# The recurrence of a hybrid encoder step: one copy of the front's rows for both halves, in three buffers

## The chip, the cores and the metric

The kernel is one launch on one core of a Trainium2 chip. The metric is the device time of the launch in microseconds (us); lower is better. PE is TensorE's matmul row and PEld its weight loads, DVE is VectorE, ACT is ScalarE, POOL is GpSimd. SP issues most DMAs.

## What is computed

A trunk of one layer runs over 2,048 tokens of a new stream and 16 tokens of each of eight running streams, all in float32. The input is normed and modulated, projected, mixed by two recurrences side by side, projected back, and sent through a mixture of experts. The change is in the recurrences:

```python
# HGRN2, 4 heads of 128 x 128:
#   S_t = diag(f_t) S_{t-1} + k_t v_t^T,   o_t = S_t^T q_t
# RWKV-7, 8 heads of 64 x 64:
def step(S, inp):
    r_t, lw_t, k_t, v_t, kk_t, a_t = inp
    sa = jnp.einsum('bhij,bhj->bhi', S, -kk_t)
    S = (S * jnp.exp(lw_t)[:, :, None, :]
         + sa[..., None] * (kk_t * a_t)[:, :, None, :]
         + v_t[..., None] * k_t[:, :, None, :])
    y = jnp.einsum('bhij,bhj->bhi', S, r_t)
    return S, y
```

Both outputs are normed by head, gated and laid side by side as `mix`, 1,024 wide.

## The kernel before

The program has four stages, one behind the other: `project`, `recur`, `merge` and `experts`. `project` leaves its results in HBM, with the channels on the rows: `rk`, for each group of 128 channels five kinds of rows (`RK_A0`, `RK_A1`, `RK_B0`, `RK_B1`, `RK_V`), `hk` with ten, and `tm`, by token. `recur` works through 17 tiles of 128 tokens, each made of two chunks of 64. Tiles 0 to 15 are the prompt; tile 16 (`TAIL`) holds the eight running streams.

A tile goes through two halves. The **front** of tile f needs no state: from `rkf` it turns V, B0 and B1 into token order (`turn`), multiplies B0 and B1 with A0 and A1 (`products`), and solves a triangular system by levels (`make_y`, `turn_x`, `make_x`), with the scores of the HGRN2 heads from `hkf` put between them (`score`). The **back** of tile b brings in the state: `from_state` multiplies A0 with the state, `solve` and `to_state` carry the state on, `y_from_state` multiplies A1 with it, and VectorE makes `mix`. The loop runs the front of tile i together with the back of tile i-1 in an order written out by hand, the same on each engine. I call one turn of this loop step i: it begins when the scores and the last transposes of the turn before are done.

The tiles of data have two buffers each, by the parity of the tile: `rkf` (all five kinds of rk, 10 KB in each partition), `hkf` (20 KB), and for the back `arb` (A0 and A1 once more, 4 KB), `qbb` and `tmb`. The front reads `rkf[f % 2]`. A whole step later the back reads A0 and A1 of the same tile, when `rkf[f % 2]` already belongs to another tile, so it has them loaded a second time into `arb`.

All of these loads are issued by SP, in the order of its program, and each waits at SP until its buffer is free:

```python
for i in range(TAIL + 1):
    if i + 2 <= TAIL:
        eng.wait_ge(ev("product_made"), 4 * i + 4)
        load_rk(i + 2)
        eng.wait_ge(ev("kd_made"), i + 1)
        load_hk(i + 2)
    b = i - 1
    if b >= 0:
        eng.wait_ge(ev("mixed"), b + 1)
        ...
```

`product_made` counts PE's products of the front, which come early in a step; `kd_made` is the last transposes of a front, and marks the end of a step; `mixed` is DVE's last operation on the mix of a tile, just behind it. By the clock a step thus begins with hk for the step after, the store of `mix`, the back's loads (`load_back`), and then rk for two steps ahead.

Of the tail, `ard`, `qbd`, `vd`, `hd` and `SAd` are masked copies that lie in buffers no longer needed (`hkf[1]` and `rkf[1]`). ScalarE writes the squares of o to `osq` and of y to `ysq`, and DVE sums them.

Of the kernel before, what the change touches and what calls it, by code (L numbers as in the profile page):

```python
# [21 lines left out]
PT = SEQ // 128  # L22
# [864 lines left out]
def recur(nc, t, bonus, ends):  # L887

    names = []
    with ExitStack() as ctx:  # L890
# [10 lines left out]

        const = sb("const", [128, N_CONST, 128])
# [4 lines left out]
        rkf = [sb(f"rkf{p}", [128, 4, N_RK, 128]) for p in range(2)]  # L907
        hkf = [sb(f"hkf{p}", [128, 4, N_HK, 128]) for p in range(2)]
        arb = [sb(f"arb{p}", [128, 4, 2, 128]) for p in range(2)]
# [17 lines left out]
        osq = sb("osq", [128, 512])  # L927
# [3 lines left out]
        ysq = sb("ysq", [128, 512])  # L931
# [12 lines left out]
        hd = [rkf[1][:, n, 0:4, :].rearrange("p a b -> p (a b)") for n in range(2)]  # L944
        SAd = [rkf[1][:, 2 + n, 0:4, :].rearrange("p a b -> p (a b)") for n in range(2)]
# [9 lines left out]

        TAIL = PT
# [8 lines left out]
        def chunk(c):  # L965
            return slice(CH * c, CH * c + CH)
# [43 lines left out]
        def _(eng):  # L1010
            eng.dma_start(ident, t["const"][:, 128 * C_ID:128 * C_ID + 128]).then_inc(ev("ident_in"), 16)

            def load_rk(f):

                k, p = 128 * f, f % 2
                for c in range(4):
                    eng.dma_start(rkf[p][:, c, :, :], rk3[:, c, :, k:k + 128]).then_inc(ev(f"rk_in{p}"), 16)
# [11 lines left out]
            def load_back(f):  # L1029

                k, p = 128 * f, f % 2
                for c in range(4):
                    eng.dma_start(arb[p][:, c, :, :], rk3[:, c, RK_A0:RK_A1 + 1, k:k + 128]).then_inc(ev(f"back_in{p}"), 16)
                eng.dma_start(qbb[p][:, :, :], hk3[:, :, HK_B, k:k + 128]).then_inc(ev(f"back_in{p}"), 16)
                eng.dma_start(tmb[p][:, :, :].rearrange("p a b -> p (a b)"), t["tm"][k:k + 128, :]).then_inc(ev(f"back_in{p}"), 16)
# [7 lines left out]
            load_back(1)  # L1043
            eng.dma_start(even[:, :, :].rearrange("p a b -> p (a b)"), t["even"]).then_inc(ev("state_in"), 16)
# [5 lines left out]
            for i in range(TAIL + 1):  # L1050
                if i + 2 <= TAIL:
                    eng.wait_ge(ev("product_made"), 4 * i + 4)
                    load_rk(i + 2)
                    eng.wait_ge(ev("kd_made"), i + 1)
                    load_hk(i + 2)
                b = i - 1
                if b >= 0:
                    eng.wait_ge(ev("mixed"), b + 1)
                    eng.dma_start(t["mix"][128 * b:128 * b + 128, :], mix[b % 2][:, :]).then_inc(ev(f"mix_out{b % 2}"), 16)
                    if b + 2 <= TAIL:  # L1060
                        load_back(b + 2)
# [17 lines left out]
        def _(eng):  # L1079
# [3 lines left out]
            def h_update(b):  # L1083

                p = b % 2
                eng.wait_ge(ev(f"back_in{p}"), 96 * (b // 2 + 1))
# [95 lines left out]
            def turn(f, kind, bank):  # L1182

                p = f % 2
                for c in range(4):
                    ins = eng.transpose(bank[:, 128 * c:128 * c + 128], rkf[p][:, c, kind, :], ident)
                ins.then_inc(ev("tok_made"), 1)

            def product(f, kind, banks, h, c):

                p, o = f % 2, 128 * (h // 2)
                return eng.matmul(banks[h % 2][chunk(c), o:o + 128].rearrange("p (a b) -> p a b", a=2), rkf[p][half(h), h // 2, kind, chunk(c)],
                                  rkf[p][half(h), h // 2, RK_A0:RK_A1 + 1, chunk(c)], start=(h < 2), stop=(h >= 6), skip_group_check=True)
# [129 lines left out]
            for i in range(TAIL + 1):  # L1323
# [8 lines left out]
                eng.wait_ge(ev(f"rk_in{p}"), 64 * (f // 2 + 1))  # L1332
# [137 lines left out]
        def _(eng):  # L1470
# [46 lines left out]
            for i in range(TAIL + 1):  # L1517
# [9 lines left out]
                if back:  # L1527
                    eng.wait_ge(ev("o_made"), b + 1)
                    eng.activation(osq[:, :], P_O[:, :], ACT.Square).then_inc(ev("o_squared"), 1)
# [11 lines left out]
                for lv in range(2, levels(f)):  # L1541
                    if back and lv == 5:
                        y_root(b)
                    keep_xt(f, lv - 1)
                    if back and lv == min(4, levels(f) - 1):
                        eng.wait_ge(ev("y_centred"), b + 1)
                        eng.activation(ysq[:, :], yc[:, :], ACT.Square).then_inc(ev("y_squared"), 1)
                    if lv < levels(f) - 1:
                        keep_x(f, lv)
# [11 lines left out]
            eng.activation(osq[:, :], P_O[:, :], ACT.Square).then_inc(ev("o_squared"), 1)  # L1561
# [13 lines left out]
            eng.activation(ysq[:, :], yc[:, :], ACT.Square).then_inc(ev("y_squared"), 1)  # L1575
# [9 lines left out]
        def _(eng):  # L1585
# [89 lines left out]
            def o_variance(b):  # L1675

                eng.wait_ge(ev("o_squared"), b + 1)
                step(eng.tensor_reduce(hst[:, 0, :], heads(osq[:, :], 4), AX.X, ALU.add))
                settle()
                eng.tensor_scalar(hst[:, 1, :], hst[:, 0, :], 1.0 / 128, NORM_EPS, ALU.mult, ALU.add).then_inc(ev("o_var"), 1)  # L1680
# [26 lines left out]
            def y_variance(b):  # L1707

                eng.wait_ge(ev("y_squared"), b + 1)
                step(eng.tensor_reduce(rst[:, 1, :], heads(ysq[:, :], 8), AX.X, ALU.add))  # L1710
# [67 lines left out]
            eng.wait_ge(ev(f"back_in{p}"), 96 * (TAIL // 2 + 1))  # L1778
# [841 lines left out]
```

## Time and profile before

| | |
|---|---|
| median of 3 runs | 3234.86 us (3229.3 to 3235.49) |
| the profiled execution | 3231.98 us |
| its span | 3230.2 us |
| PE busy | 2943.0 us, 91% |
| PEld busy | 1735.1 us, 54% |
| DVE, ACT, POOL busy | 44%, 30%, 5% |
| bytes moved by DMA | 575.75 MB, mean 178 GB/s |
| mean granted clock of TensorE | 0.956 |
| stage `recur` | about 1107 to 1800 us |

The span is the time from the first to the last instruction that the profile holds; the execution's own time is 1.8 us longer. "Busy" adds up the instructions of an engine; the weight loads run beside the matmuls. A wait is given with its releaser, the engine and line that ended it; "issue" stands where the profile shows nothing that was waited for.

### The profile page before, as it was taken

Reading aid. Unit: us, or ns where it says so; the run is one execution under the profiler, and the core shown is the slowest. Engines: PE = TensorE matmul, PEld = TensorE weight load, DVE = VectorE, ACT = ScalarE, POOL = GpSimd, SP = SyncE. Lnnn points to the kernel's source line nnn. Section 1 sums busy time; section 2 is a strip of 40 time slices with the busy share of each in tenths; the row PEclk is TensorE's granted clock in tenths of the full one; section 3 lists DMA queues with packets and bytes.
Section 4 is the critical chain, followed back from the end, with each engine's and each line's share of the span. In section 5 each row is a group of like instructions: output and inputs, shape, how many; then the busy total and the mean of one; then the engine's idle time right before and its main releaser. Section 6 shows DMA issues by size and latency. Waiting matters only on the chain. (4 is left out here: it accounts for less than half of the span.)

```text
span 3230.2 us, 68743 instructions
## 1 busy us (share of the span) xinstructions
PE 2943.0 (91%) x28939; PEld 1735.1 (54%) x28940; DVE 1410.5 (44%) x3438; ACT 974.7 (30%) x1872; POOL 162.0 (5%) x248
## 2 busy tenths in 40 slices
PE   6998999999999488888898599949999999999988
PEld 2432455454555378778787355535555555555543
DVE  2245466665655545666666144451221122212217
ACT  2456334343334223333332122102222212222215
POOL 0000000000000000000000000001011001111104
PEclk8999999999999789999999699979999999999998
DMA  7531123242332586555661643465786478767758
GB/s 270 209 130 56 50 93 116 92 138 85 109 132 86 163 220 181 155 153 156 173 181 37 213 162 115 152 170 205 286 323 255 152 262 308 254 230 276 253 196 332
DMA packets 373371, 575.75 MB, mean 178 GB/s; under 512 B 31246, under 2 KB 231110, under 8 KB 370088
## 3 DMA queue, kind: packets, MB, share of 16 engines
q1 hardware_dynamic: 335112, 470.72, 43.2%
q0 software_dynamic: 18080, 72.10, 6.4%
q10 hardware_dynamic: 19968, 29.83, 3.2%
q8 instruction: 168, 2.75, 0.4%
q14 instruction: 43, 0.35, 0.0%
HBM read 427.04 MB, written 145.54 MB: 177 GB/s over the span
## 5 line engine op out<-in xcount | busy, mean ns | idle before, releaser
L451 PE MATMUL pj_P<-pj_hT,pj_wc 128*128 128x448 f32 (+2 forms) x1600 | 592.0, 517 | 0.9 <-ACT pj_stage L579 0.9
L2493 PE MATMUL moe_PG<-wgu,moe_xT 128*64 128x256 f32 x5248 | 582.1, 380 | 0.7 <-ACT moe_xT L2391 0.7
L2493 PEld LDWEIGHTS moe_PG<-wgu,moe_xT 128*64 128x64 f32 x5248 | 377.5, 137 | 226.0 <-issue 47.2
L451 PEld LDWEIGHTS pj_P<-pj_hT,pj_wc 128*128 128x128 f32 x1600 | 294.8, 189 | 257.5 <-issue 241.2
L2500 PE MATMUL moe_PTY<-wd,moe_hT 128*64 128x512 f32 x1312 | 317.7, 603 | 0.0
L2394 ACT ACT_TABLE_LOAD x82 | 105.2, 1283 | 483.1 <-issue 483.0
L1978 PE MATMUL merge_PO<-merge_w,merge_mT 128*128 128x512 f32 x544 | 240.9, 601 | 1.6 <-DMA merge_w<-in_w_out 1.6
L1978 PEld LDWEIGHTS merge_PO<-merge_w,merge_mT 128*128 128x128 f32 x544 | 103.3, 192 | 126.6 <-issue 123.9
L2357 DVE COPY moe_hT<-moe_PH 128x128 f32<-128x128 f32 x164 | 47.8, 292 | 281.0 <-PE moe_PH L2485 281.0
L2353 DVE TENSOR_TENSOR moe_sg<-moe_sg,moe_PG 128x128 f32<-128x128 f32 x164 | 46.4, 283 | 282.7 <-ACT moe_sg L2394 282.7
L2360 DVE COPY moe_y<-moe_PTY 128x512 f32<-128x512 f32 x82 | 56.7, 692 | 208.3 <-PE moe_PTY L2500 208.3
L2500 PEld LDWEIGHTS moe_PTY<-wd,moe_hT 128*64 128x64 f32 x1312 | 81.9, 136 | 120.2 <-issue 86.8
L372 PE MATMUL pj_P<-pj_wt,pj_hT 128*128 128x512 f32 x272 | 122.9, 606 | 0.0
L482 PE MATMUL pj_P<-pj_wt,pj_hT 128*128 128x512 f32 x272 | 121.3, 599 | 0.0
L1300 PE MATMUL re_P<-re_hkf 128*64 128x64 f32 x1872 | 87.6, 237 | 10.7 <-issue 9.6
L600 ACT ACTIVATE pj_rk<-pj_P,pj_keep_mu 128x448 f32<-128x448 f32 (+1 forms) x60 | 35.9, 602 | 196.8 <-DVEq L866 91.6
L2396 ACT ACTIVATE moe_sg<-moe_PG 128x128 f32<-128x128 f32 x82 | 22.8, 278 | 234.3 <-PE moe_PG L2493 234.3
L1655 DVE COPY_PREDICATED re_Y<-re_const,re_P 128x256 f32<-128x256 uint32 x166 | 64.5, 442 | 54.9 <-PE re_P L1251 28.4
L1508 ACT COPY re_XT<-re_P 128x256 f32<-128x256 f32 x132 | 42.7, 375 | 148.2 <-PE re_P L1260 148.2
L482 PEld LDWEIGHTS pj_P<-pj_wt,pj_hT 128*128 128x128 f32 x272 | 50.3, 190 | 67.7 <-issue 67.7
L2441 POOL DMA_INDIRECT moe_xg<-scratch_h,moe_row x83 | 80.6, 971 | 67.1 <-POOL moe_row L2438 67.1
L372 PEld LDWEIGHTS pj_P<-pj_wt,pj_hT 128*128 128x128 f32 x272 | 51.8, 196 | 59.8 <-issue 59.8
(385 smaller groups left out, 4140.2 us busy)
## 6 DMA issues: line engine op xcount, KB each, us to landing
wgu<-in_w_gate SPq DMA_DIRECT2D x32, 2048.0 KB, 9.4
wgu<-in_w_up SPq DMA_DIRECT2D x32, 2048.0 KB, 15.0
wd<-in_w_down SPq DMA_DIRECT2D x32, 2048.0 KB, 16.6
re_hkf<-scratch_hk SPq DMA_DIRECT2D x60, 640.0 KB, 8.0
re_rkf<-scratch_rk SPq DMA_DIRECT2D x68, 320.0 KB, 6.6
scratch_hk<-pj_hk SPq DMA_DIRECT2D x16, 1344.0 KB, 5.8
scratch_y_rows<-moe_y ACTq DMA_DIRECT2D x164, 128.0 KB, 5.2
scratch_rk<-pj_rk SPq DMA_DIRECT2D x16, 1120.0 KB, 4.4
```

Source lines behind the costliest of these rows:

```text
L372: ins = eng.matmul(P[2 + m % 2][:, :], hT_cols(m)[:, k, :], wt[:, k, :], start=(k == 0), stop=(k == KD - 1))
L451: ins = eng.matmul(bank[:, 0:wp], wc[:, j, k, :], hT[:, k, k0:k0 + wp], start=(k == 0), stop=(k == KD - 1), skip_group_check=True)
L482: ins = eng.matmul(PQ[:, :], rows[:, k, :], wt[:, k, :], start=(k == 0), stop=(k == KD - 1))
L1300: ins = eng.matmul(P_ST[chunk(c), 256 + 64 * h:320 + 64 * h], hkf[p][:, h, a, chunk(c)], hkf[p][:, h, b, chunk(c)], start=(h == 0), stop=( ...
L1655: eng.copy_predicated(Y[lv - 1][:, 4 * g:4 * g + 4, :], level_mask(C_LEVEL_T, lv).bitcast(U32).unsqueeze(1).to_broadcast([128, 4, CH]), he ...
L1978: ins = eng.matmul(PO[:, half, :], mT[:, n % 2, k, :], w[:, k, 512 * half:512 * half + 512], start=(k == 0), stop=(k == KD - 1))
L2357: eng.tensor_copy(hT[:, j, :], PH[:, j, 0:128]).then_inc(ev("hT_kept"), 1)
L2360: eng.tensor_copy(y[:, :], PY[:, :]).then_inc(ev("y_kept"), 1)
L2394: eng.activation(sg[:, 0, :], PG[:, 0, 0:128], ACT.Sigmoid).then_inc(ev("sigmoid_made"), 1)
L2441: eng.indirect_dma_start(xg[:, :], None, t["h2"].rearrange("t (h c) -> (t h) c", h=2), bass.IndirectOffsetOnAxis(ap=row[:, 0:1], axis=0)). ...
L2493: ins = eng.matmul(PG[64 * c:64 * c + 64, j, 0:256].rearrange("p (a b) -> p a b", a=2), x_rows, wgu[p][:, :, k, o:o + 128], start=(k == 0) ...
L2500: ins = eng.matmul(PY[64 * n:64 * n + 64, :], hT[:, j, 64 * c:64 * c + 64], wd[p][:, 2 * c + j, 512 * n:512 * n + 512], start=(j == 0 and ...
```

## The change

- `rkf` has three buffers, chosen by `f % 3`, with a semaphore for each; `arb` is gone. `from_state` and `y_from_state` of the back read `RK_A0` and `RK_A1` in `rkf[b % 3]`, and so does the masked copy `ard` of the tail.
- `load_back` loads `qbb` and `tmb` only, so `back_in` counts 32 a tile, not 96.
- `load_rk(2)` is issued at the start, ahead of the running streams' states. In the loop `load_rk(i + 2)`, behind the fourth product, becomes `load_rk(b + 3)`, the same tile, behind the store of `mix` of tile b = i - 1 and ahead of `load_back`.
- `osq` and `ysq` are one buffer, `sq`. `hd` and `SAd` lie in `rkf[(TAIL + 1) % 3]`.

The SBUF space: a third `rkf` takes 10 KB a partition, `arb` gave back 8 KB and the squares 2 KB.

```diff
+        TAIL = PT
...
-        rkf = [sb(f"rkf{p}", [128, 4, N_RK, 128]) for p in range(2)]
+        rkf = [sb(f"rkf{p}", [128, 4, N_RK, 128]) for p in range(3)]
         hkf = [sb(f"hkf{p}", [128, 4, N_HK, 128]) for p in range(2)]
-        arb = [sb(f"arb{p}", [128, 4, 2, 128]) for p in range(2)]
...
-        osq = sb("osq", [128, 512])
+        sq = sb("sq", [128, 512])
...
-        ysq = sb("ysq", [128, 512])
...
-        hd = [rkf[1][:, n, 0:4, :].rearrange("p a b -> p (a b)") for n in range(2)]
-        SAd = [rkf[1][:, 2 + n, 0:4, :].rearrange("p a b -> p (a b)") for n in range(2)]
+        hd = [rkf[(TAIL + 1) % 3][:, n, 0:4, :].rearrange("p a b -> p (a b)") for n in range(2)]
+        SAd = [rkf[(TAIL + 1) % 3][:, 2 + n, 0:4, :].rearrange("p a b -> p (a b)") for n in range(2)]
...
-                    eng.dma_start(rkf[p][:, c, :, :], rk3[:, c, :, k:k + 128]).then_inc(ev(f"rk_in{p}"), 16)
+                    eng.dma_start(rkf[f % 3][:, c, :, :], rk3[:, c, :, k:k + 128]).then_inc(ev(f"rk_in{f % 3}"), 16)
...
-                for c in range(4):
-                    eng.dma_start(arb[p][:, c, :, :], rk3[:, c, RK_A0:RK_A1 + 1, k:k + 128]).then_inc(ev(f"back_in{p}"), 16)
                 eng.dma_start(qbb[p][:, :, :], hk3[:, :, HK_B, k:k + 128]).then_inc(ev(f"back_in{p}"), 16)
...
             load_back(1)
+            load_rk(2)
             eng.dma_start(even[:, :, :].rearrange("p a b -> p (a b)"), t["even"]).then_inc(ev("state_in"), 16)
...
             for i in range(TAIL + 1):
                 if i + 2 <= TAIL:
-                    eng.wait_ge(ev("product_made"), 4 * i + 4)
-                    load_rk(i + 2)
                     eng.wait_ge(ev("kd_made"), i + 1)
                     load_hk(i + 2)
                 b = i - 1
                 if b >= 0:
                     eng.wait_ge(ev("mixed"), b + 1)
                     eng.dma_start(t["mix"][128 * b:128 * b + 128, :], mix[b % 2][:, :]).then_inc(ev(f"mix_out{b % 2}"), 16)
+                    if b + 3 <= TAIL:
+                        load_rk(b + 3)
                     if b + 2 <= TAIL:
                         load_back(b + 2)
...
-                    ins = eng.matmul(out_g(chunk(c), h), arb[p][half(h), h // 2, 0, chunk(c)], ST[half(h), h // 2, :],
+                    ins = eng.matmul(out_g(chunk(c), h), rkf[b % 3][half(h), h // 2, RK_A0, chunk(c)], ST[half(h), h // 2, :],
...
-                    ins = eng.matmul(out_y(chunk(c), h), arb[p][half(h), h // 2, 1, chunk(c)], ST[half(h), h // 2, :],
+                    ins = eng.matmul(out_y(chunk(c), h), rkf[b % 3][half(h), h // 2, RK_A1, chunk(c)], ST[half(h), h // 2, :],
...
-                eng.wait_ge(ev(f"rk_in{p}"), 64 * (f // 2 + 1))
+                eng.wait_ge(ev(f"rk_in{f % 3}"), 64 * (f // 3 + 1))
...
-                step(eng.tensor_tensor(ard[n][:, :, :, :].rearrange("p m a c -> p (m a) c"), arb[p][:, :, :, :].rearrange("p m a c -> p (m a) c"),
-                                       cols.unsqueeze(1).to_broadcast([128, 8, 128]), ALU.mult))
+                step(eng.tensor_tensor(ard[n][:, :, :, :], rkf[TAIL % 3][:, :, RK_A0:RK_A1 + 1, :],
+                                       cols.unsqueeze(1).unsqueeze(1).to_broadcast([128, 4, 2, 128]), ALU.mult))
```

What moves is on SP alone; PE, DVE, ACT and POOL have the same instructions in the same order. First SP's start, from the back's loads of the second tile to the first store of `mix` (`even`, `even_row`, `Sd` and `srow` are the masks and the states of the running streams). Before:

```order
L1033 DMA re_arb1<-scratch_rk 128x2x128 x4
L1034 DMA re_qbb1<-scratch_hk 128x4x128
L1035 DMA re_tmb1<-scratch_tm 128x1536
L1044 DMA re_even<-in_even 128x256
L1045 DMA re_even_row<-in_even_row 128x2
L1046 DMA re_Sd<-in_state_hgrn 128x32x128
L1049 DMA re_srow<-in_state_rwkv 64x8x64 x8
L1017 DMA re_rkf0<-scratch_rk 128x5x128 x4
L1024 DMA re_hkf0<-scratch_hk 128x10x128 x4
L1017 DMA re_rkf1<-scratch_rk 128x5x128 x4
L1024 DMA re_hkf1<-scratch_hk 128x10x128 x4
L1059 DMA scratch_mix<-re_mix0 128x1024
```

After the change:

```order
L1031 DMA re_qbb1<-scratch_hk 128x4x128
L1032 DMA re_tmb1<-scratch_tm 128x1536
L1016 DMA re_rkf2<-scratch_rk 128x5x128 x4
L1042 DMA re_even<-in_even 128x256
L1043 DMA re_even_row<-in_even_row 128x2
L1044 DMA re_Sd<-in_state_hgrn 128x32x128
L1047 DMA re_srow<-in_state_rwkv 64x8x64 x8
L1023 DMA re_hkf0<-scratch_hk 128x10x128 x4
L1023 DMA re_hkf1<-scratch_hk 128x10x128 x4
L1055 DMA scratch_mix<-re_mix0 128x1024
```

rk of tile 2 (`rkf2`) now stands ahead of the states, and the two rk loads that stood around the first `hkf0` of the loop are gone from there. The other place is one step in the middle of the loop. Before:

```order
L1024 DMA re_hkf0<-scratch_hk 128x10x128 x4
L1059 DMA scratch_mix<-re_mix1 128x1024
L1033 DMA re_arb1<-scratch_rk 128x2x128 x4
L1034 DMA re_qbb1<-scratch_hk 128x4x128
L1035 DMA re_tmb1<-scratch_tm 128x1536
L1017 DMA re_rkf1<-scratch_rk 128x5x128 x4
L1024 DMA re_hkf1<-scratch_hk 128x10x128 x4
```

After the change:

```order
L1023 DMA re_hkf0<-scratch_hk 128x10x128 x4
L1055 DMA scratch_mix<-re_mix1 128x1024
L1016 DMA re_rkf1<-scratch_rk 128x5x128 x4
L1031 DMA re_qbb1<-scratch_hk 128x4x128
L1032 DMA re_tmb1<-scratch_tm 128x1536
L1023 DMA re_hkf1<-scratch_hk 128x10x128 x4
```

The four `arb` loads are gone, and the four rk loads that came last in the step stand between the store of `mix` and the loads of `qbb` and `tmb`.

## Rows read from the trace of the kernel before

**Rows 1.** The page: busy time of each engine, and the instruction queue (packets, MB, share).
```profile
PE 2943.0 (91%) x28939; PEld 1735.1 (54%) x28940; DVE 1410.5 (44%) x3438; ACT 974.7 (30%) x1872; POOL 162.0 (5%) x248
...
q8 instruction: 168, 2.75, 0.4%
```

**Rows 2.** Windows: us, busy (count) of PE, PEld, DVE, ACT, POOL; PEclk, DMA share, GB/s.
```profile
1107.00:1161.00 54.00, 29.26 (x720) 25.91 (x722) 14.10 (x35) 9.39 (x22) 0.00 (x0) 0.69 1.09 284
1161.00:1681.00 520.00, 461.59 (x13654) 417.31 (x13650) 317.49 (x724) 168.31 (x433) 0.00 (x0) 0.97 0.60 165
1681.00:1715.00 34.00, 32.17 (x980) 28.97 (x980) 23.13 (x54) 12.08 (x31) 0.00 (x0) 1.00 0.42 127
```

**Rows 3.** Waits of PE in steps 1 to 14: total us, times, longest us.
```profile
PE re_P L1251 <- issue: 10.2, 5, 2.8
PE re_P L1300 <- issue: 9.6, 9, 3.2
...
PE re_P L1240 <- issue: 0.2, 1, 0.2
```

**Rows 4.** Windows from one resumption of PE to the next, behind a burst.
```profile
1405.69:1409.71 4.02, 3.36 (x128) 3.02 (x128) 1.23 (x3) 1.29 (x4) 0.00 (x0) 1.00 0.02 5
1409.71:1413.83 4.12, 3.23 (x128) 2.75 (x127) 2.90 (x7) 1.80 (x5) 0.00 (x0) 1.00 0.02 4
```

**Rows 5.** Timeline of SP, one step: start us, us, issue.
```profile
1420.41 5.44 SPq L1024 DMA_DIRECT2D re_hkf<-scratch_hk  x4
1425.90 2.98 SPq L1059 DMA_DIRECT2D scratch_mix<-re_mix  x1
1428.92 3.04 SPq L1033 DMA_DIRECT2D re_arb<-scratch_rk  x4
1432.00 0.47 SPq L1034 DMA_DIRECT2D re_qbb<-scratch_hk  x1
1432.51 1.09 SPq L1035 DMA_DIRECT2D re_tmb<-scratch_tm  x1
1433.65 4.73 SPq L1017 DMA_DIRECT2D re_rkf<-scratch_rk  x4
```

**Rows 6.** Timeline of PE at the end of the gap: start us, us, work, idle before.
```profile
1441.59 0.58 PE L1251 MATMUL re_P<-re_X,re_LB 64*64 64x64 f32 x10 [2.84 <-issue]
```

**Rows 7.** DMA view of the burst, 1420.4 to 1442.4 us.
```profile
DMA packets 9709, 6.08 MB, mean 276 GB/s; under 512 B 239, under 2 KB 9450, under 8 KB 9706
q1 hardware_dynamic: 9706, 6.03, 99.5%
```

**Rows 8.** DMA view, 1434.5 to 1438.5, then 1438.5 to 1439.0 us.
```profile
DMA packets 1077, 1.25 MB, mean 313 GB/s; under 512 B 41, under 2 KB 949, under 8 KB 1077
q1 hardware_dynamic: 1077, 1.25, 99.6%
...
q8 instruction: 1, 0.02, 14.7%
```

**Rows 9.** Windows behind the gap of rows 6.
```profile
1442.00:1445.00 3.00, 3.00 (x87) 2.77 (x81) 1.54 (x4) 0.65 (x2) 0.00 (x0) 0.50 0.05 14
1445.00:1450.00 5.00, 4.75 (x188) 4.20 (x180) 3.62 (x9) 1.94 (x6) 0.00 (x0) 1.00 0.02 3
```

**Rows 10.** The tile rkf: what PE waited for (us, times), and its loads' time to land.
```profile
  DMA re_rkf<-scratch_rk: 26.4, 1
DMA to landing us min/median/max: 4.5/6.6/12.4
```

**Rows 11.** Step 1: SP's two rk loads, and PE's two gaps.
```profile
1161.29 3.46 SPq L1017 DMA_DIRECT2D re_rkf<-scratch_rk  x4
1172.92 6.52 SPq L1017 DMA_DIRECT2D re_rkf<-scratch_rk  x4
...
1179.32 0.27 PE L1135 MATMUL re_PEO<-re_ST,re_arb 64*64 64x64 f32 x2 [1.54 <-issue]
1184.27 0.91 PE L1177 MATMUL re_PEO<-re_SA,re_LB 64*64 64x64 f32 x24 [1.89 <-issue]
```

More of the change, by code:

```diff
@@ L943, in recur @@
         vd = [hkf[1][:, 2 + n, 4:8, :].rearrange("p a b -> p (a b)") for n in range(2)]
-        hd = [rkf[1][:, n, 0:4, :].rearrange("p a b -> p (a b)") for n in range(2)]
-        SAd = [rkf[1][:, 2 + n, 0:4, :].rearrange("p a b -> p (a b)") for n in range(2)]
+        hd = [rkf[(TAIL + 1) % 3][:, n, 0:4, :].rearrange("p a b -> p (a b)") for n in range(2)]
+        SAd = [rkf[(TAIL + 1) % 3][:, 2 + n, 0:4, :].rearrange("p a b -> p (a b)") for n in range(2)]
         P_A, P_B, P_C, P_D, P_ST, P_O = [ctx.enter_context(nc.psum_tensor(f"re_P{b}", [128, 512], F32)) for b in range(6)]
         P_EO = ctx.enter_context(nc.psum_tensor("re_PEO", [128, 2, 512], F32))
-        TAIL = PT
         AHEAD = {2: (), 3: (1,), 4: (3,), 5: (5,)}
@@ L1085, in h_update @@
                 p = b % 2
-                eng.wait_ge(ev(f"back_in{p}"), 96 * (b // 2 + 1))
+                eng.wait_ge(ev(f"back_in{p}"), 32 * (b // 2 + 1))
                 eng.wait_ge(ev("kdT_kept"), b + 1)
@@ L1185, in turn @@
                 for c in range(4):
-                    ins = eng.transpose(bank[:, 128 * c:128 * c + 128], rkf[p][:, c, kind, :], ident)
+                    ins = eng.transpose(bank[:, 128 * c:128 * c + 128], rkf[f % 3][:, c, kind, :], ident)
                 ins.then_inc(ev("tok_made"), 1)
@@ L1191, in product @@
                 p, o = f % 2, 128 * (h // 2)
-                return eng.matmul(banks[h % 2][chunk(c), o:o + 128].rearrange("p (a b) -> p a b", a=2), rkf[p][half(h), h // 2, kind, chunk(c)],
-                                  rkf[p][half(h), h // 2, RK_A0:RK_A1 + 1, chunk(c)], start=(h < 2), stop=(h >= 6), skip_group_check=True)
+                return eng.matmul(banks[h % 2][chunk(c), o:o + 128].rearrange("p (a b) -> p a b", a=2), rkf[f % 3][half(h), h // 2, kind, chunk(c)],
+                                  rkf[f % 3][half(h), h // 2, RK_A0:RK_A1 + 1, chunk(c)], start=(h < 2), stop=(h >= 6), skip_group_check=True)
             def products(f, kind, banks):
@@ L1528, in _ @@
                     eng.wait_ge(ev("o_made"), b + 1)
-                    eng.activation(osq[:, :], P_O[:, :], ACT.Square).then_inc(ev("o_squared"), 1)
+                    eng.activation(sq[:, :], P_O[:, :], ACT.Square).then_inc(ev("o_squared"), 1)
                 eng.wait_ge(ev("x0_made"), f + 1)
@@ L1546, in _ @@
                         eng.wait_ge(ev("y_centred"), b + 1)
-                        eng.activation(ysq[:, :], yc[:, :], ACT.Square).then_inc(ev("y_squared"), 1)
+                        eng.activation(sq[:, :], yc[:, :], ACT.Square).then_inc(ev("y_squared"), 1)
                     if lv < levels(f) - 1:
@@ L1560, in _ @@
             eng.wait_ge(ev("o_made"), TAIL + 1)
-            eng.activation(osq[:, :], P_O[:, :], ACT.Square).then_inc(ev("o_squared"), 1)
+            eng.activation(sq[:, :], P_O[:, :], ACT.Square).then_inc(ev("o_squared"), 1)
             eng.wait_ge(ev("as_made"), 2 * TAIL + 1)
@@ L1574, in _ @@
             eng.wait_ge(ev("y_centred"), TAIL + 1)
-            eng.activation(ysq[:, :], yc[:, :], ACT.Square).then_inc(ev("y_squared"), 1)
+            eng.activation(sq[:, :], yc[:, :], ACT.Square).then_inc(ev("y_squared"), 1)
             eng.wait_ge(ev("y_var"), TAIL + 1)
@@ L1677, in o_variance @@
                 eng.wait_ge(ev("o_squared"), b + 1)
-                step(eng.tensor_reduce(hst[:, 0, :], heads(osq[:, :], 4), AX.X, ALU.add))
+                step(eng.tensor_reduce(hst[:, 0, :], heads(sq[:, :], 4), AX.X, ALU.add))
                 settle()
@@ L1709, in y_variance @@
                 eng.wait_ge(ev("y_squared"), b + 1)
-                step(eng.tensor_reduce(rst[:, 1, :], heads(ysq[:, :], 8), AX.X, ALU.add))
+                step(eng.tensor_reduce(rst[:, 1, :], heads(sq[:, :], 8), AX.X, ALU.add))
                 settle()
@@ L1777, in _ @@
             p = TAIL % 2
-            eng.wait_ge(ev(f"back_in{p}"), 96 * (TAIL // 2 + 1))
+            eng.wait_ge(ev(f"back_in{p}"), 32 * (TAIL // 2 + 1))
             eng.wait_ge(ev("state_in"), 16 * (3 + NSEQ))
```

## The prediction

> **What bounds the kernel now.** I read the page first. TensorE is busy 91% of the span [rows 1]; the change touches one of four stages, the recurrence, so I cut that stage by its own clock. The table of windows [rows 2] gives its step 0 (1107 to 1161 us), steps 1 to 14 (1161 to 1681) and step 15 (1681 to 1715). In the 520 us of steps 1 to 14 the matmul row is busy 461.59 us, so TensorE paces the loop, and 58.4 us are idle: 37.1 us a step.
>
> The table of waits says what that idle time is. Almost none of it waits for another engine: the largest entries carry the releaser "issue", that is, for nothing that the profile shows [rows 3]; all thirteen such entries come to 48.9 us, 3.5 us a step. What they are is read from where they fall. Two resumptions after such a gap are 1405.70 and 1409.71, the next is 1413.84, and each interval holds 128 matmuls and as many weight loads, one short in one record [rows 4]. So TensorE stops after equal amounts of program, not at a given tensor. The queue called instruction moved 168 packets, 2.75 MB, 16 KB each [rows 1], and one packet goes for each such piece. These gaps are TensorE waiting for its own program. Between 1405.69 and 1413.83 data traffic is nil (share 0.02) and a piece still takes 4.0 to 4.1 us: the floor of that supply.
>
> Next the traffic. SP issues a step's loads in one go, from 1420.41 to 1438.4 [rows 5] (phase, below, is the time since the first of them), and the 22 us from there move 9,706 packets and 6.03 MB at 99.5% of the 16 engines [rows 7]. The rest of the step is empty (share 0.60 over the whole, [rows 2]). The large gap comes inside that burst: 2.84 us, ending at 1441.59 [rows 6]. From 1434.5 to 1438.5 all 1,077 packets are the data queue's, among them the 128 long rows of tmb (1,077 less the 949 under 2 KB); the packet that ends the wait went between 1438.5 and 1439.0 [rows 8]. So **the data burst delays the program, and TensorE pays**. After the gap the granted clock is 0.50 for 3 us (1.2 GHz of 2.4), 87 matmuls against 188 in the next 5 us [rows 9]: 29 per us for 37.6, some 0.7 us lost on top. The mean clock of 0.97 over 520 us [rows 2] makes 31 us at the lower level, ten such spells in fourteen steps.
>
> The proof by absence is step 15, which asks for no rk rows: share 0.42 of 34 us, 14.3 us busy instead of 22.3, and it lasts 33.9 us, 3.2 less than the mean step [rows 2].
>
> **The change part by part.**
> *The second read of A0 and A1 goes.* Four loads of 128 KB a step, 1,024 packets of 512 B, of 6.03 MB and 9,706 packets [rows 7]. By bytes at the 276 GB/s of that row 0.524 MB is 1.9 us, by packets 22 x 0.995 x 1,024 / 9,706 = 2.3 us. I take 2.0 us off each burst. What a shorter burst is worth has two bounds. Step 15 gives the lower: 8 us less burst gave 3.2 us, 0.4 per us, so 0.8 us a step. The upper is one for one, 2.0 us, since the gap ends about where the burst ends (21.2 us after the first issue, of a burst of some 22). I take **1.1 us** a step: 0.8 plus 0.3 for the clock (ten spells of 0.7 us are 0.5 a step; of these something over half should go with smaller gaps). It is nearer the lower bound, since step 15 is the nearest row, and since the packet that ends the gap goes some 3 us before the burst's end, where a burst cut by 2 us hardly reaches it.
>
> *The front's rk rows move.* Today they are the last loads of a step, for two steps ahead; now they come between the store of mix and the rows of qbb and tmb, for one step ahead. On SP four issues for four: rk (4.73 us) comes in, arb (3.04 us) goes out ahead of qbb and tmb [rows 5]. These two land some 2 to 4 us later, by about phase 20, and are wanted by the next step's first matmuls, at phase 37: covered by 17 us. rk is issued from phase 8.5 (5.44 + 2.98) and lands within 12.4 us at worst [rows 10], by 21 to 26, and the transposes of the next step want it: covered by over 10 us. Today TensorE waits for rk exactly once, at the very start, 26.4 us [rows 10], where its four loads stand first on SP before and after: nothing. If that cover were gone every step would wait; it would take a burst twice as long. SP's wait for the fourth product goes; behind it only rk stood. The wait on mixed has hk ahead of it and rk, qbb and tmb behind, and mixed is done by 1425.9, while hk is still being issued, so nobody waits for it longer than now.
>
> *Step 1 is relieved.* There two rk loads are issued today, at 1161.29 and 1172.92, and TensorE stops for 1.54 and 1.89 us at 1179.32 and 1184.27 [rows 11]. Now rk for step 2 goes ahead of the states during step 0 and rk for step 3 to step 2: **-3.0 us** of the 3.4. Step 0 trades two arb loads (-1.05 MB) for one of rk (+1.31 MB) in 54 us that are saturated anyway (284 GB/s, [rows 2]): 0, give or take 2.
>
> *Step 15 is loaded.* It now asks for the rows of step 16: +4.5 us of rk for -2 us of arb, at 0.4 to 1 per us +1 to +2.5; I take **+1.5 us**.
>
> *Squares, hd, SAd, the masked A rows.* One buffer for both squares: ScalarE writes the second only after y is centred, three levels after the first was summed, and both engines keep that order. The two masks read the same elements with another stride, and hd and SAd move to the buffer that is free. PE, DVE and ACT have the same rows in the same order, so the pieces of program break at the same matmuls. All 0, hidden or unchanged.
>
> Sum: -3.0 - 13 x 1.1 + 1.5 = **-15.8 us** on the profiled execution's 3231.98, so 3216; that execution stands 2.9 us under the median of 3234.86. Against the median: 3219; between the two I say **3218 us**. A measurement here tells some 0.2%, 6.5 us, from no change.
>
> The Trainium skill speaks against this ("Runtime: NRT & Kernel Launch", "Instruction fetch mechanics"): fetching is streamed ahead and hidden behind the issue of instructions. By that rule the gaps would be something else and the sum nothing. The trace disagrees: [rows 4] and [rows 8].
>
> **The rivals.**
> *The burst's end is what ends the gap.* For it: the end of the gap lies at 21.2 us in the step shown, and of a burst's length only the last part touches a gap. Then each step gains 2.0 us and the clock: -3 - 13 x 2.2 + 2.5 = -29, **3206 us**. Against it: step 15's 0.4 per us.
>
> *The loads are hidden; nothing moves.* The gap is set by which piece of program meets a full queue, and a step with 20 us of burst has as many pieces in it as one with 22. Then -3 + 1.5: **3233 us**. For it: gaps of 0.7 us also come with no traffic at all, at 1409.71 [rows 4], and a piece cannot come faster than 4.0 us; what is won in the burst can be lost behind it.
>
> *Slower: the long rows now stand last.* tmb's packets (6 KB) pass between phase 14 and 18 now, and no instruction packet passes beside them [rows 8]. After the change hk, mix, rk are issued with no lighter load between them and tmb closes the burst, just where the step's third piece is wanted. If a piece that asks at phase 16 must sit out rk's rest and tmb, its gap grows by about the length of tmb, 0.79 MB at 276 GB/s = 2.8 us, in the one step of three where the pieces fall so, less what the shorter burst saves (0.8): +2.0 x 13/3 = +9, and step 15 +2.5, step 1 -3: +8.2, **3243 us**. It decides from the point where the main gap's mean passes today's 3.5 us a step. The Trainium skill ("DMA: Bandwidth & Descriptors", "Queues, rings and completion order") lets an engine switch between queues only after a whole packet of several descriptors, which is this mechanism; by the trace such waits exist [rows 8].
>
> **How the numbers follow.** Forecast 0.52, one for one 0.14, hidden 0.21, slower 0.13. The forecast's own range, with 0.8 to 1.7 us a step, is 3208 to 3225. The range to hold 8 in 10 reaches into both neighbours: **3203 to 3237**. Faster by over 0.2% takes the forecast and the first rival, 0.66; within 0.2% the hidden one and the edges, 0.22; slower 0.12.
>
> **What would show it.** Right: no arb loads, 5.5 MB and some 20 us busy in a step's burst; "issue" gaps in steps 2 to 14 down from 3.5 to about 2.4 us a step; step 1 near 34 us, step 15 near 35.5; still one wait of TensorE for rk. Wrong: a second such wait; gaps as long as before at the burst's new end; or gaps that merely move behind tmb.

## The result, and the profile after

| | before | changed |
|---|---|---|
| median | 3235.49 us (5 runs, 3229.3 to 3245.67) | 3217.3 us (5 runs, 3215.24 to 3221.84) |
| ratio | | 0.9938, 95% interval 0.9920 to 0.9957 |
| profiled execution | 3231.98 us | 3221.84 us |
| its span | 3230.2 us | 3220.0 us |

The change makes the kernel faster by 18 us, 0.6%. The forecast was 3218 us. The total came out as forecast; the largest part, steps 2 to 14, was given its gain for the wrong reason, as the experiments show.

The profiled execution of the changed kernel is the slowest of its five. Behind the recurrence, from the first matmul of `merge` on, it takes 2.9 us longer than that of before, in code that is the same (before, then changed):

```profile
1809.95:3230.18 1420.23, 1332.86 (x8696) 706.16 (x8696) 418.39 (x1136) 309.62 (x568) 130.20 (x201) 0.97 0.65 232
```
```profile
1796.83:3220.00 1423.17, 1332.25 (x8696) 705.54 (x8696) 418.47 (x1136) 309.59 (x568) 129.88 (x201) 0.97 0.65 231
```

So the stage is read by itself. A step is cut at the first matmul that brings the values of HGRN2 into the state (`h_update`); columns as in [rows 2]. Step 1, steps 2 to 14 and step 15 before:

```profile
1161.90:1199.10 37.20, 32.91 (x980) 30.00 (x976) 20.85 (x50) 12.08 (x31) 0.00 (x0) 0.95 0.59 150
1199.10:1682.10 483.00, 428.88 (x12692) 387.48 (x12688) 297.70 (x677) 156.82 (x403) 0.00 (x0) 0.97 0.60 166
1682.10:1716.00 33.90, 32.07 (x980) 28.89 (x977) 23.03 (x53) 12.08 (x31) 0.00 (x0) 1.00 0.43 128
```

and in the changed kernel:

```profile
1163.10:1196.20 33.10, 31.39 (x980) 28.69 (x976) 20.99 (x50) 12.07 (x31) 0.00 (x0) 1.00 0.35 91
1196.20:1665.20 469.00, 423.87 (x12692) 381.06 (x12688) 297.99 (x677) 156.73 (x403) 0.00 (x0) 0.99 0.57 156
1665.30:1701.60 36.30, 32.38 (x978) 29.13 (x976) 23.07 (x53) 12.07 (x31) 0.00 (x0) 1.00 0.50 141
```

Steps 2 to 14 go from 483.0 to 469.0 us with the same 12,692 matmuls, step 1 from 37.2 to 33.1, step 15 from 33.9 to 36.3. Of the 14.0 us, 9.0 are idle time (54.1 us against 45.1 beside the matmul row) and 5.0 are busy time. I put that to the clock: the work is the same, and the mean granted clock rises from 0.97 to 0.99.

The waits of TensorE in the same 520 us as [rows 3] (total us, times, longest us):

```profile
PE re_P L1258 <- issue: 7.2, 10, 1.7
PE re_P L1298 <- issue: 6.7, 13, 0.9
PE re_P L1249 <- issue: 4.7, 8, 0.9
```

The entries "issue" come to 38.3 us where there were 48.9, and these 520 us now hold part of step 15 as well. In steps 2 to 14 alone they fall from 45.3 to 36.1 us, 3.5 to 2.8 a step, and to 32.5 us (2.5 a step) in the second profile of the change, `change_again` below. L1298 and L1249 are the L1300 and L1251 of before; their longest wait was 3.2 and 2.8 us and is 0.9 in this profile. Long gaps are not gone: one of 2.6 us is left, and the second profile has one of 2.9. SP's step, which answers to [rows 5]:

```profile
1409.60 5.44 SPq L1023 DMA_DIRECT2D re_hkf<-scratch_hk  x4
1415.08 3.63 SPq L1055 DMA_DIRECT2D scratch_mix<-re_mix  x1
1418.76 3.88 SPq L1016 DMA_DIRECT2D re_rkf<-scratch_rk  x4
1422.68 1.67 SPq L1031 DMA_DIRECT2D re_qbb<-scratch_hk  x1
1424.39 0.83 SPq L1032 DMA_DIRECT2D re_tmb<-scratch_tm  x1
```

The burst, to compare with [rows 7], in the 22 us from the first issue:

```profile
DMA packets 8628, 5.57 MB, mean 253 GB/s; under 512 B 176, under 2 KB 8368, under 8 KB 8624
q1 hardware_dynamic: 8624, 5.51, 91.5%
```

0.52 MB and 1,082 packets fewer, and 91.5% of the window in place of 99.5%, 20.1 us. And the tile `rkf`, to compare with [rows 10]:

```profile
  DMA re_rkf<-scratch_rk: 26.8, 1
DMA to landing us min/median/max: 4.7/5.9/14.1
```

One wait for rk, at the start, as before: the cover held.

### The profile page after: what moved, and what is told of

It is laid out like the page before. It is cut to its first block and busy times, and to the rows that moved or that the text cites. A ratio compares the mean times of both kernels' runs of the same rounds, so it can differ in the third digit from the quotient of the medians.

```text
span 3220.0 us, 68675 instructions
## 1 busy us (share of the span) xinstructions
PE 2938.7 (91%) x28939; PEld 1728.7 (54%) x28940; DVE 1411.6 (44%) x3438; ACT 974.2 (30%) x1872; POOL 161.3 (5%) x248
## 5 line engine op out<-in xcount | busy, mean ns | idle before, releaser
L2392 ACT ACT_TABLE_LOAD x82 | 105.2, 1283 | 483.0 <-issue 482.9
L600 ACT ACTIVATE pj_rk<-pj_P,pj_keep_mu 128x448 f32<-128x448 f32 (+1 forms) x60 | 35.9, 602 | 196.8 <-DVEq L866 91.7
L1298 PE MATMUL re_P<-re_hkf 128*64 128x64 f32 x1872 | 86.6, 234 | 7.8 <-issue 6.7
```

The costliest lines, as they stand in the source:

```text
L1298: ins = eng.matmul(P_ST[chunk(c), 256 + 64 * h:320 + 64 * h], hkf[p][:, h, a, chunk(c)], hkf[p][:, h, b, chunk(c)], start=(h == 0), stop=( ...
L2392: eng.activation(sg[:, 0, :], PG[:, 0, 0:128], ACT.Sigmoid).then_inc(ev("sigmoid_made"), 1)
```

## The experiments

Single profiled executions of one kernel differ by 5 to 10 us, so totals are compared by ratios, each with the kernel before on the same chip, and stages by several profiles. A second quantity is worked out from the trace. [rows 4] showed that TensorE's program comes in pieces of 256 instructions, one packet of the instruction queue for each. **The delay** below is the time from TensorE's first instruction of a piece to the start of the next packet of that queue, averaged over the pieces that begin in a given part of steps 2 to 14. With no data in flight it is 1.0 to 1.4 us.

The delay decides a gap. In the eight profiles of the kernel before, the change, `rk_last`, `arb_kept` and `rk_last_short` (the last three are explained below) TensorE has 244 gaps of over 0.3 us at the end of a piece in these steps. It resumes 2.5 us (median; all lie between 2.2 and 3.0) after the start of the packet, in each profile alike. So a piece takes its delay plus 2.5 us, or TensorE's own work on it where that is longer, and a gap is what the delay has over.

### Amount or place: two kernels that each do half of the change

The texts recorded ahead of the runs name the theories by letter: A, only the amount of traffic counts; B, only the place of the loads in the step; C, both; D, the long rows of tmb are what holds up the program.

`rk_last` keeps the three buffers and the lost arb loads, and puts rk back at the end of the step:

```diff
-                    if b + 3 <= TAIL:
-                        load_rk(b + 3)
                     if b + 2 <= TAIL:
                         load_back(b + 2)
+                    if b + 3 <= TAIL:
+                        load_rk(b + 3)
```

> The changed kernel with one thing put back: in the loop the rk loads stand last again, behind qbb and tmb; arb stays gone. Before, a step of steps 2 to 14 lasted 37.15 us, with the change 36.08. Theory A (only the amount of traffic counts): steps of 36.1 us, total as the changed kernel, about 3217 to 3219 us. Theory B (only the place of the long tmb rows counts, the lost arb traffic is worth nothing): steps of 37.1 us, total about 3231. Theory C (both count, as in the forecast: what delays the program is what stands in the DMA queues when TensorE asks for the next piece): between them, 36.4 to 36.8 us a step, total 3222 to 3227. Main gap of the step behind phase 14 back to 2 us or more under B, about 1 us under A.

`arb_kept` is the kernel before, with two buffers and arb, and rk ahead of the back's loads:

```diff
+                if i == 0:
+                    eng.wait_ge(ev("product_made"), 4)
+                    load_rk(2)
                 if i + 2 <= TAIL:
-                    eng.wait_ge(ev("product_made"), 4 * i + 4)
-                    load_rk(i + 2)
                     eng.wait_ge(ev("kd_made"), i + 1)
...
+                    if b + 3 <= TAIL:
+                        load_rk(b + 3)
                     if b + 2 <= TAIL:
                         load_back(b + 2)
```

> The kernel before with one thing changed: rk is issued between the store of mix and the back's loads, two buffers, arb still loaded (rk of tile 2 still in step 0 to 1, rk of tile 3 a step later). Theory A (amount only): steps 2 to 14 stay at 37.15 us, step 1 gains about 2 to 3 us and step 15 loses 2, total about 3234. Theory B (order only): steps of 36.1 us, total about 3220. Theory C (both): 36.5 to 36.9 us, total 3226 to 3231. If arb_kept and rk_last together give more or less than the change's 1.07 us a step, the two effects do not add.

The first time `rk_last` came to 0.9966 (0.9954 to 0.9978), 3229.33 against 3237.89 us, and `arb_kept` to 0.9930 (0.9908 to 0.9951), 3218.19 us from four runs. Both were run again beside the changed kernel, on one chip.

> The changed kernel once more, beside the next three on one chip, since single profiled executions of one kernel differ by some 5 to 10 us: 0.9938 again, some 20 us under the kernel before.

> rk last in the step, arb gone (traffic alone). First time 0.9966. If the place of the loads counts for about half, it lies 9 us over the changed kernel again, ratio 0.996 to 0.9975; if the first result was chance and only the amount counts, it meets the changed kernel at 0.994.

> rk ahead of the back's loads, arb kept (place alone). First time 0.9930 from 4 runs, as good as the whole change. Theory B (place alone is the change): 0.993 to 0.995 again, and the lost 8.9 MB of arb are worth under 4 us. Theory C (both): 0.996.

| one chip, before 3233.6 us | median us | ratio (95%) | steps 2 to 14 in its profile |
|---|---|---|---|
| the change (no arb, rk ahead) | 3211.78 | 0.9936 (0.9913 to 0.9959) | 465.3 us |
| rk_last (no arb, rk last) | 3228.47 | 0.9984 (0.9971 to 0.9997) | 477.8 us |
| arb_kept (arb, rk ahead) | 3222.54 | 0.9958 (0.9940 to 0.9976) | 477.7 us |

The lost traffic alone is worth 5 us by the medians (9 the first time), the new place alone 11 us (20 the first time), the two together 22 us. The changed kernel and `rk_last` differ in nothing but the order of six loads in a step, their intervals do not meet, and the medians lie 17 us apart. So theory A falls. By the medians place counts for most of it, but theory B does not hold in full: with arb kept the second time some 11 us are missing, though the intervals of these two overlap, and the two halves together (16 us) give less than the whole (22). How the sum divides is known no better than to these intervals. The single profiles divide it otherwise: in the table the two halves gain alike, and the first profiles had 485.2 us for `rk_last` and 475.4 for `arb_kept`. Two profiles of one kernel thus lie up to 7.4 us apart in these 13 steps. In profiles, `change_again`, `rk_last_again` and `arb_kept_again`:

```profile
1192.70:1658.00 465.30, 423.22 (x12692) 380.71 (x12688) 298.15 (x677) 156.66 (x403) 0.00 (x0) 0.99 0.57 158
```
```profile
1198.30:1676.10 477.80, 429.48 (x12692) 388.01 (x12688) 297.46 (x677) 156.75 (x403) 0.00 (x0) 0.97 0.56 153
```
```profile
1195.10:1672.80 477.70, 428.44 (x12691) 385.55 (x12689) 297.51 (x677) 156.81 (x403) 0.00 (x0) 0.98 0.61 168
```

### Why the place counts: the long rows of tmb

A step's piece that begins at phase 12 to 15 (phase: us from about the step's first hk issue) had to wait 3.2 us for the next packet in the kernel before (2.8 to 3.5 by where the edges of the bin are put), 3.6 and 3.7 in the two profiles of `rk_last`, but 2.1 and 2.0 in the two of the change and 2.1 in both of `arb_kept`, eight to ten pieces each. What passes then is tmb, with rows of 6 KB, in the slow ones, and rk, with rows of 512 B, in the others.

The long rows are not gone from the other kernels, they pass later. By their packets they go at phase 14 to 18 before, 12 to 16 in `rk_last`, 17 to 20 in the change, and 19 to 22 in `arb_kept`, where arb stands ahead of them. There the twelve pieces of the two profiles that begin at phase 18 to 19 wait 3.1 us, and the eleven of the change 1.3. So arb costs something by pushing tmb into that part of the step, and amount and place are not two separate terms.

`rk_last_short` takes `rk_last` and cuts tmb's rows:

```diff
-                eng.dma_start(tmb[p][:, :, :].rearrange("p a b -> p (a b)"), t["tm"][k:k + 128, :]).then_inc(ev(f"back_in{p}"), 16)
+                for j in range(6):
+                    eng.dma_start(tmb[p][:, :, :].rearrange("p a b -> p (a b)")[:, 256 * j:256 * j + 256], t["tm"][k:k + 128, 256 * j:256 * j + 256]).then_inc(ev(f"back_in{p}"), 16)
```

> rk last as in rk_last, but tmb in six loads with rows of 1 KB in place of one with rows of 6 KB. In the profile of rk_last a piece of program that TensorE asked for at phase 9 to 15, with tmb in the queues, came 3.6 us later on average, against 2.1 to 2.8 in the changed kernel, where rows of 512 B pass at that phase. Theory D (the long rows hold up the program's packets): with short rows the delay falls to under 3 us and the kernel gets within 3 us of the changed one, about 0.994 to 0.995. If it is not the length of the rows but what is queued in all: as rk_last, 0.9966, or slower for five more issues a step.

Same bytes, same order, five more issues a step: 0.9943 (0.9923 to 0.9963), 3214.57 us against the 3228.47 of `rk_last` beside it and 2.8 us over the change. The delay at phase 12 to 15 is 1.7 us. That is what theory D said. One thing changes beside the length of the rows: one load becomes six, which SP issues over some 4 us in place of 1. Six loads with long rows were not tried, so this rival is not excluded. In one step, where both kernels stand at the same piece: first `rk_last_again`, SP's issues, then the DMA view from the start of a piece at 1322.1 us to 1325.7, then the half microsecond after it, then TensorE's gap.

```profile
1317.46 0.44 SPq L1031 DMA_DIRECT2D re_qbb<-scratch_hk  x1
1317.94 0.88 SPq L1032 DMA_DIRECT2D re_tmb<-scratch_tm  x1
1318.87 5.84 SPq L1016 DMA_DIRECT2D re_rkf<-scratch_rk  x4
```
```profile
DMA packets 1732, 1.16 MB, mean 321 GB/s; under 512 B 49, under 2 KB 1680, under 8 KB 1731
q1 hardware_dynamic: 1731, 1.15, 110.3%
...
q8 instruction: 1, 0.02, 15.1%
```
```profile
1328.39 0.28 PE L1249 MATMUL re_P<-re_X,re_LB 64*64 64x64 f32 x3 [2.14 <-issue]
```

In 3.6 us no packet of TensorE's instruction queue (q8) goes; of the 1,731 packets of data 51 are long. Then `rk_last_short`, from the same piece at 1310.6 us:

```profile
1305.21 0.44 SPq L1031 DMA_DIRECT2D re_qbb<-scratch_hk  x1
1305.68 4.37 SPq L1033 DMA_DIRECT2D re_tmb<-scratch_tm  x6
1310.09 2.83 SPq L1016 DMA_DIRECT2D re_rkf<-scratch_rk  x4
```
```profile
DMA packets 1075, 0.68 MB, mean 282 GB/s; under 512 B 57, under 2 KB 1075, under 8 KB 1075
q1 hardware_dynamic: 1075, 0.68, 98.2%
...
q8 instruction: 1, 0.02, 12.6%
```
```profile
1315.44 0.28 PE L1250 MATMUL re_P<-re_X,re_LB 64*64 64x64 f32 x3 [0.76 <-issue]
```

The packet goes after 2.4 us in place of 3.6, and the gap before the same matmul (`make_y` of level 2, the same three left of it) is 0.76 us in place of 2.14.

The Trainium skill ("DMA: Bandwidth & Descriptors", "Queues, rings and completion order") says that an engine changes queue only after a packet of several descriptors. The runs agree as far as they go: the same bytes in shorter rows, in six loads, let the instruction queue in earlier. They do not show how many rows make up such a turn.

### Less in a step, or the same spread over it

`no_rk` leaves out rk for tiles 3 to 15:

```diff
                 for c in range(4):
-                    eng.dma_start(rkf[f % 3][:, c, :, :], ...)
+                    if f < 3 or f == TAIL:
+                        eng.dma_start(rkf[f % 3][:, c, :, :], ...)
...
-                eng.wait_ge(ev(f"rk_in{f % 3}"), 64 * (f // 3 + 1))
+                eng.wait_ge(ev(f"rk_in{f % 3}"), 64 * (2 if f == TAIL else 1))
```

> The changed kernel, except that rk is loaded for tiles 0, 1, 2 and 16 alone: tiles 3 to 15 work on the rows of an earlier tile, so their results are of other data. Only the recurrence's steps are read, since the routing behind it may change. 4.5 us less burst a step. At step 15's slope of 0.4 us for each us, steps 2 to 14 fall by 1.8 us from 35.9 (the mean of two profiles of the change) to 34.1 us. If traffic counts only by its place, less: 35. If one for one: 33.0 or below, where the supply without traffic (4.0 us a piece, 7.7 pieces a step, 30.8 us) no longer binds.

Steps 2 to 14:

```profile
1192.10:1649.40 457.30, 422.73 (x12690) 380.62 (x12688) 298.29 (x677) 156.66 (x403) 0.00 (x0) 0.99 0.43 123
```

35.2 us a step against 35.9, the mean of the change's two profiles. The share of DMA falls from 0.57 to 0.43, 20.4 to 15.1 us a step, so 5.3 us less traffic bring 0.7 us: 0.14 for each, and not the 0.4 that step 15 of the kernel before had suggested. 34.1 was expected. Both ends are single profiles: with the 7.4 us by which two profiles of `rk_last` differ the price could be 0.25, still under 0.4. So with the order of the change the rk traffic is worth little. (The total, 3258.58 us, is not compared, since the experts do other work: 29,369 matmuls for 28,939.)

`second_half` lets rk and the back's loads wait for the middle of the step:

```diff
+                    if b + 2 <= TAIL:
+                        eng.wait_ge(ev("xt_made"), before(b + 2, 4) + 1)
                     if b + 3 <= TAIL:
                         load_rk(b + 3)
```

> The changed kernel, but rk and the back's loads wait at SP until the running front's first turned X is made (about phase 19 of the step), so that a step has two short bursts, of some 12 and 8 us, and a pause between them. The bytes are the same. If the gaps are the program waiting behind queued data, a pause lets the supply catch up: no gap of over 1 us, steps of 35 us or less, 14 us off the total, 3203 us. If the amount of traffic in a step decides, steps stay at 36.1 us. If rk or tmb now come too late, TensorE shows waits for DMA at the start of each step and the total rises over 3217.

`paced` puts waits for events of the running front ahead of hk's second to fourth load, of rk's first and third, of qbb and of tmb:

```diff
+                    if c and f >= 2:
+                        eng.wait_ge(ev(("tok_made", "product_made", "product_made")[c - 1]), (3 * (f - 1) + 2, 4 * (f - 1) + 2, 4 * (f - 1) + 4)[c - 1])
...
+                    if f >= 3 and c == 0:
+                        eng.wait_ge(ev("x0_made"), f)
+                    if f >= 3 and c == 2:
+                        eng.wait_ge(ev("y_made"), before(f - 1, 5) + 1)
...
+                if f >= 2:
+                    eng.wait_ge(ev("y_made"), before(f, 5) + 2)
                 eng.dma_start(qbb[p][:, :, :], ...)
+                if f >= 2:
+                    eng.wait_ge(ev("y_made"), before(f, 5) + 3)
```

> The changed kernel, with SP's loads of a step spread over it: the four hk loads each behind an event of the running front, then rk in two pairs, qbb, tmb. Same bytes, same buffers. If queued data delays the program, shallow queues bring most of the rest: steps of 34.5 us or less (step 15 of the kernel before, with 14 us of burst, took 33.9), total about 3197 to 3203. If the amount decides, 36.1 us a step. If bytes per step is what matters to nothing but the burst's end, the result lies with second_half. A wait of TensorE for hkf or rkf would show that the pace is too slow.

Both missed what was expected. `second_half` is at 0.9984 (0.9972 to 0.9997), 3234.14 us, and its 13 steps last 480.0 us; `paced` at 0.9948 (0.9932 to 0.9964), 3220.2 us, 476.3. In neither does TensorE wait for hkf or rkf in the loop. `paced` does what it should in the first part of the step: the delay of pieces that begin at phase 0 to 9 falls from 2.4 to 4.8 us in the change to 1.4 to 1.7. But there TensorE had time: in the change it takes 5 to 7 us over a piece that begins at phase 0 to 9, and no large gap stood there. From phase 18 on it takes about 4, hardly more than a piece needs to come with no data at all (4.0 us, [rows 4]), and loads in flight there show as gaps. In `second_half` the delay at phase 18 to 26 (21 pieces) is 2.4 to 3.2 us where the change has 1.2 to 1.4. One step of `paced`, tmb at 1364.09:

```profile
1339.49 10.16 SPq L1029 DMA_DIRECT2D re_hkf<-scratch_hk  x4
1349.70 2.06 SPq L1065 DMA_DIRECT2D scratch_mix<-re_mix  x1
1352.20 4.78 SPq L1020 DMA_DIRECT2D re_rkf<-scratch_rk  x4
1357.90 0.36 SPq L1039 DMA_DIRECT2D re_qbb<-scratch_hk  x1
1364.09 0.33 SPq L1042 DMA_DIRECT2D re_tmb<-scratch_tm  x1
```
```profile
1360.67 0.57 PE L1308 MATMUL re_P<-re_hkf 128*64 128x64 f32 x13 [2.10 <-issue]
1370.50 1.13 PE L1268 MATMUL re_P<-re_const,re_X 64*64 64x64 f32 x30 [2.31 <-issue]
```

`second_half` lost nearly the whole gain: its interval does not meet the change's. `paced` cannot be told from the change (0.9938 and 0.9936); that spreading loses is not shown, only that it brings nothing that can be seen. What matters is what is still queued when TensorE begins to need a piece every 4 us.

### Versions that might beat both

`short` is the changed kernel with tmb in rows of 1 KB, `short_mix` has the store of mix in rows of 1 KB too:

```diff
-                    eng.dma_start(t["mix"][128 * b:128 * b + 128, :], mix[b % 2][:, :]).then_inc(ev(f"mix_out{b % 2}"), 16)
+                    for j in range(4):
+                        eng.dma_start(t["mix"][128 * b:128 * b + 128, 256 * j:256 * j + 256], mix[b % 2][:, 256 * j:256 * j + 256]).then_inc(ev(f"mix_out{b % 2}"), 16)
```

and `short_states` has `short`'s rows and takes the running streams' states out of the start:

```diff
-            eng.dma_start(Sd[:, :, :, :], t["state_hgrn"][0].rearrange("s h k v -> k s h v")).then_inc(ev("state_in"), 16)
...
+                    if 1 <= b <= 4:
+                        for s in range(2 * b - 2, 2 * b):
+                            eng.dma_start(Sd[:, s, :, :], t["state_hgrn"][0, s].rearrange("h k v -> k h v")).then_inc(ev("state_in"), 16)
+                    if 5 <= b <= 12:
+                        s = b - 5
+                        o = slice(RW_N * (s % 2), RW_N * (s % 2) + RW_N)
+                        eng.dma_start(srow[o, s // 2, :].rearrange("v (h k) -> v h k", k=RW_N), ...)
```

> The changed kernel (tmb last in the step), with tmb in six loads with rows of 1 KB. rk_last_short was 0.9943, within 3 us of the change. Theory D (long rows hold up the program's packets while they are in the queues): the end of the burst gets lighter too, pieces asked for at phase 15 to 18 come in under 2.3 us for now 2.3 to 2.9, 0.2 to 0.4 us a step, ratio 0.992 to 0.993. If only the place in the step mattered, no gain: 0.9936 as the change.

> As short, and the store of mix (rows of 4 KB, at phase 10 to 12) in four stores with rows of 1 KB. Theory D: the delay at phase 9 to 12 falls from 2.6 to 2.8 us to about 2.0, another 0.2 us a step, ratio 0.991 to 0.992. If stores are another matter than loads, or three more issues on SP cost as much: as short.

> As short, and the masks and states of the running streams (3.1 MB, needed in the tail alone) are loaded one small piece a step in steps 2 to 14 instead of in step 0, where the DMA engines are full for all of its 41 us. Step 0 has gaps of some 7 us in total: it should fall to about 36 us, minus 4 to 5 us, and each later step pays for 0.13 to 0.5 MB more, at 0.4 to 0.5 us for each us of traffic (0.5 to 1.8 us) some 0.2 to 0.8 us for twelve steps, plus 3 to 6 us. Sum near nothing, 0.992 to 0.994. If the place in the step counts for more than that, since these come last in it, slower than short by more than 5 us.

| one chip, before 3234.51 us | median us | ratio (95%) |
|---|---|---|
| short | 3211.43 | 0.9930 (0.9912 to 0.9948) |
| short_mix | 3215.53 | 0.9941 (0.9919 to 0.9963) |
| short_states | 3205.99 | 0.9915 (0.9896 to 0.9934) |

In its profile `short` has the shortest steps of all kernels that load everything, 459.0 us for thirteen. The delay at phase 15 to 18 fell as expected, from 2.3 and 2.7 us in the change to 1.7. But its total cannot be told from the change's 0.9936; whether short rows still win anything with tmb last stays open. Cutting mix's rows brought nothing that can be told either. `short_states` has the lowest median, 29 us under the kernel before; that it beats `short` is likely and not shown, since the intervals overlap. Its first stretch, step 0, and its step 15:

```profile
1122.00:1155.40 33.40, 26.34 (x737) 23.15 (x738) 10.93 (x25) 8.11 (x21) 0.00 (x0) 0.86 1.00 263
1652.80:1690.50 37.70, 32.80 (x978) 29.29 (x976) 23.07 (x53) 12.08 (x31) 0.00 (x0) 1.00 0.48 136
```

Step 0 takes 33.4 us for 39.7 in `short`, the nearest kernel, and 41 to 42 in the change's two profiles. But `rk_last` has the change's step 0 to the letter and shows 36.6 and 39.4, so the states cost it some 3 to 8 us; that this is more than the 4 to 5 expected is not shown. Steps 2 to 14, which took most of them over, last 464.1 us for `short`'s 459.0 and give back part of it.

## Why the prediction was right, and where it was not

- **What bounds the stage** was read rightly. TensorE's "issue" gaps are waits for its own program: they end 2.5 us after the packet, whatever the kernel. And data delays that program: cutting tmb's rows, with the same bytes, moved the total by 14 us. The Trainium skill's rule ("Runtime: NRT & Kernel Launch", "Instruction fetch mechanics"), by which such fetches stay hidden, does not hold in this loop: the gaps come to 45.3 us in steps 2 to 14 before.
- **Steps 2 to 14**, forecast 1.1 us each: 1.07 in the first profile (37.15 to 36.08), 1.36 in the second (35.79). The size was right, the reason was not, and that the sum met it is luck. The text made it of 0.8 us for the shorter burst, 0.3 for the clock, and priced the move of rk within a step at nothing. By that, `rk_last` should have been as fast as the change and `arb_kept` should have won about what step 1 gives. The runs showed nearly the reverse: the shorter burst by itself is worth 5 to 9 us over the whole kernel, the move by itself 11 to 20. The step that failed is the slope of 0.4 us for each us of traffic, taken from step 15 alone; `no_rk` measured 0.14. Step 15 differs from a middle step in more than rk. It also loads less hk (eight small loads of tile 16 for four large ones): 4.29 MB in all for 6.08, and rk is only 1.31 of the difference. And its pieces begin elsewhere. Which of these made it fast was not tried; that its burst ended before TensorE needs its pieces fast is my reading. The slope was too high and the move was left out, and the two errors cancelled.
- **The gaps** of steps 2 to 14 were to fall from 3.5 to about 2.4 us a step and fell to 2.8 and 2.5.
- **The clock** was taken at something over half of ten spells in fourteen steps. The trace has eight (one of them twice as long as the others), and one or two after the change. The mean clock of steps 2 to 14 went from 0.97 to 0.99 and busy time fell by 5.0 us, 0.39 a step for 0.3.
- **Step 1**, forecast -3.0: 37.2 to 33.1, -4.1, and 33.9 in the second profile, -3.3.
- **Step 15**, forecast +1.5: 33.9 to 36.3 and 35.6, +2.4 and +1.7. The rival's term, +2.5, fits as well.
- **Step 0**, forecast 0, give or take 2: 40.4 to 41.0 and 41.9, +0.6 and +1.6.
- **Sum of the stage**, from the first matmul to the start of step 16: 594.5 to 579.5 and 576.7 us, -15.0 and -17.8 for -15.8.
- **The squares, hd, SAd and the masked rows**, forecast 0: nothing in the profile speaks against it, but none of it was tried by itself.
- **The rivals.** "The loads are hidden" falls with the total. "One for one" (3206 us) falls too: with 5.3 us less traffic the steps gained 0.7. "Slower: the long rows now stand last" had the mechanism that decides and the wrong sign. It named the long rows and the one step in three whose piece begins at phase 16 to 17: such steps exist (`change_again` has gaps of over 1.5 us in them), and the longest delays left, 3.7 to 4.0 us, belong to pieces that begin at phase 16 to 17, just ahead of tmb. But I weighed only what tmb costs at the end, not what it had cost in the middle, where a piece began in eight of thirteen steps. It did cost: 3.2 us of delay before, 2.1 after.

## What to carry to other kernels

Where a long program runs straight on and its engine shows gaps with no releaser after equal numbers of instructions, look at what the DMA queues hold at that moment. Order a step's loads by that: the bulk where the engine is slow over its instructions, the long rows where it asks for no program, or cut them to 1 KB. Holding loads back into the dense part of the step cost nearly the whole gain here; spreading them brought nothing. And a slope taken from the one step that differs in several ways prices none of them: leave out one thing at a time.

## What the runs showed of the hardware that was not expected

- A piece of 256 instructions took 4.0 to 4.1 us to come with no data in flight in the kernel before, 3.7 to 4.1 in the change, while TensorE went through the fastest pieces in 3.0 us. So a stretch of small matmuls can run at the rate of its program and not of the array.
- TensorE resumed 2.5 us after the start of the packet that it waited for, in 244 gaps of eight profiles.
- Rows of 6 KB held up the instruction packet by 3.6 to 3.7 us on average, rows of 512 B by 2.0 to 2.1 and of 1 KB by 1.7 (in six loads), with the data queue at work throughout. `second_half`, with two short bursts, had a median 17 to 22 us over those of the change, measured in another series.
- A gap can drag the clock down behind it, as in [rows 9], but need not: in the kernel before the longest gap, 3.20 us, ending at 1368.06, was followed by no spell at 1.2 GHz. The only such spell in steps 2 to 14 of the changed kernel comes with its longest gap, 2.62 us:

```profile
1613.38 0.80 PE L1269 MATMUL re_P<-re_Y,re_XT 64*64 64x64 f32 x18 [2.62 <-issue]
```
```profile
1612.00:1616.00 4.00, 2.62 (x56) 2.50 (x57) 0.00 (x0) 0.65 (x2) 0.00 (x0) 0.56 0.02 4
```
